# Three of the four input pairs of the Fox value projection computed as seven block products each

## The chip, the cores and the metric

The kernel runs on one core of one Trainium2 chip. The metric is the device time of one execution in microseconds (us); lower is better. Engines are named PE (TensorE, matrix products), DVE (VectorE), ACT (ScalarE), POOL (GpSimd) and SP (the engine that issues most transfers).

## What is computed

Two transformer blocks run on 256 tokens of width 1024. The change lies in the second block's first mixer, the "Fox" attention, whose projection gives queries, keys, values, a forget logit and a gate:

```
q, k, v, f_logit, gate = _split(x @ w_in, [H * dh, H * dh, H * dh, H, D])   # H = 8, dh = 128, D = 1024
...
s = jnp.einsum('bqhd,bshd->bhqs', q_b, k).astype(jnp.float32) * scale
s = s + jnp.transpose(c_b, (0, 2, 1))[..., None] - cum_t[:, :, None, :]
s = jnp.where(kpos[None, :] <= qpos[:, None], s, -jnp.inf)
p = jax.nn.softmax(s, axis=-1).astype(v.dtype)
return jnp.einsum('bhqs,bshd->bqhd', p, v)
```

All inputs are float32. The value projection is v = x @ w_v with x 256 x 1024 and w_v 1024 x 1024.

## The kernel before

**Precision.** A float32 operand is split into a rounded part ("high", type fp32r) and the remainder ("low"). One block product is three matmuls (`three`, L484 to L486): high x high, high x low, low x high, each 128 x 128 by 128 x 512.

**Weight chunks.** Weights come as chunks of 128 partitions x 2048 floats (1 MB) through a ring of four slots, `raw`. For chunk c ACT writes the high part `whi` (`hi(c)`, L1219), then DVE writes the low part `wlo` (`lo(c)`, L1679); POOL does the low parts of the output projection's chunks (L1611). PE waits in `take(c)` for the low part. SP may load chunk c once the low part of chunk c - 4 is done, and ACT may write `whi` of c once PE has used c - 4. Every engine runs its instructions in the order written; semaphores tie the engines together.

**The stage.** The query and key chunks Q0 to Q7 (`C_FQK + h`), one head each, take 32 matmuls of 512 columns and 16 of 256 columns on PE (L519, L525) into two of four banks (4 to 7) of PSUM, so head h uses the banks of head h - 2. After each, ACT copies the right halves of both banks into `qk_sum` ("cross copy", L1460) and makes one high part; DVE adds the left halves (L2038), writes q and k (L2040, L2041) and makes one low part, of the chunk four ahead. PE starts head h only when DVE's addition of head h - 2 is done (`qk2_ready`). Then come the four value chunks (`C_FV`, 24 matmuls each in `by_tokens`), with the score matmuls of heads 0 and 1 (`scores2`, L962) ahead of the last. ACT and DVE copy the values out, scaled by the rows' norm (L1464, L1469, L2047). DVE also adds the mask to the attention bias (L2056). In the attention, for each head, PE makes scores, DVE adds the bias and takes the row maximum (`causal`, L1862), ACT takes the exponential (`exps`, L1345), PE transposes (`turn_probs`, L782), DVE copies (L1870) and PE multiplies with the values (L837 to L839). Then the output projection begins (`C_FO`).

**Seven products, as used already.** In both feed-forward down projections ten weight chunks are done by Strassen's scheme in seven block products instead of eight (`seven`). The sums of weight blocks are written by DVE (`weight_sums`, L366 to L370) into the next ring slot, so that a pair of inputs takes two slots, the second of them without a load. The first slot needs only 1536 of its 2048 columns split.

## Time and profile before

| | us |
|---|---|
| median of 3 runs | 701.61 |
| lowest, highest | 700.35, 701.9 |
| profiled execution | 700.18 |
| its span, first to last instruction | 698.4 |
| PE busy in the span | 689.4 |
| DVE busy | 544.3 |
| ACT busy | 399.2 |

The profile is of one execution. A busy time counts an instruction from its start to its end. Matmuls overlap, so that the pace is read from start to start, not from durations. "Idle before" names what released an engine. The mean granted clock of PE was 0.997 of 2.4 GHz.

### The profile page before, as it was taken

What the parts mean: (1) busy time and instruction counts of PE and PEld (TensorE: products, weight loads), DVE (VectorE), ACT (ScalarE), POOL (GpSimd) and SP (SyncE); (2) the same over time, 40 slices, a digit from 0 to 9 for tenths busy, and PEclk for the clock granted to TensorE, in tenths of its full rate; (3) what the DMA queues carried; (4) which work ended last, traced back from release to release, by engine and by line L of the source; (5) the groups of instructions that cost most, each with busy time, mean ns of one, the idle gap of its engine ahead of it and who ended that gap; (6) DMA issues with size and microseconds to landing.
All of it is one profiled execution on the core that took longest, in us unless ns stands there. A gap on an engine that the chain in (4) does not pass through costs nothing.

```text
span 698.4 us, 9915 instructions
## 1 busy us (share of the span) xinstructions
PE 689.4 (99%) x3702; PEld 588.1 (84%) x3702; DVE 544.3 (78%) x808; ACT 399.2 (57%) x533; POOL 84.4 (12%) x70
## 2 busy tenths in 40 slices
PE   8999999999999999999999999999999999999995
PEld 7888888888888788888888888888888888888885
DVE  6788788999777776877778999976763748898757
ACT  6866555556377546655555556487444625576451
POOL 0022204000000000022104000000006172140001
PEclk9999999999999999999999999999999999999998
DMA  8966653356685053755553347664663174543001
GB/s 341 367 229 232 227 193 120 121 181 242 249 330 203 1 218 152 262 181 182 184 186 139 110 172 301 234 249 173 234 249 116 74 292 133 173 158 137 1 1 60
DMA packets 21253, 129.34 MB, mean 185 GB/s; under 512 B 2520, under 2 KB 3936, under 8 KB 7008
## 3 DMA queue, kind: packets, MB, share of 16 engines
q1 hardware_dynamic: 19872, 127.51, 49.8%
q10 hardware_dynamic: 1344, 1.34, 0.6%
q8 instruction: 23, 0.38, 0.2%
q14 instruction: 14, 0.11, 0.0%
HBM read 127.79 MB, written 1.06 MB: 184 GB/s over the span
## 4 chain that ended last, share of the span: by engine, by line
PE 97%; DVE 1%; DMA 1%; issue 0%; ACT 0%; ACTq 0%; DVEq 0%
PE ps L519 25%; PE ps L484 16%; PE ps L486 16%; PE ps L485 16%; PE ps L525 13%; PE ps L504 1%; PE ps L782 1%; PE ps L678 1%; PE ps L538 1%; PE ps L1142 1%; PE ps L962 1%; PE ps L508 1%; DMA raw<-in_first 1%; PE ps L694 1%; PE ps L837 1%; PE ps L839 1%
## 5 line engine op out<-in xcount | busy, mean ns | idle before, releaser
L1219 ACT ACTIVATE whi<-raw 128x2048 fp32r<-128x2048 f32 (+1 forms) x88 | 164.6, 1873 | 69.4 <-PE ps L486 51.1
L1679 DVE TENSOR_TENSOR wlo<-raw,whi 128x2048 fp32r<-128x2048 f32 (+1 forms) x81 | 181.2, 2255 | 17.5 <-ACT whi L1219 17.4
L519 PE MATMUL ps<-xt,whi 128*128 128x512 f32 x752 | 180.1, 391 | 0.0
L519 PEld LDWEIGHTS ps<-xt,whi 128*128 128x128 f32 x752 | 138.1, 188 | 26.7
L484 PE MATMUL ps<-whi,xt 128*128 128x512 f32 (+2 forms) x340 | 134.7, 396 | 0.0
L486 PE MATMUL ps<-whi,xt 128*128 128x512 f32 (+2 forms) x340 | 130.1, 383 | 0.0
L485 PE MATMUL ps<-wlo,xt 128*128 128x512 f32 (+2 forms) x340 | 129.9, 382 | 0.0
L525 PEld LDWEIGHTS ps<-xt,wlo 128*128 128x128 f32 x752 | 96.4, 191 | 3.7
L525 PE MATMUL ps<-xt,wlo 128*128 128x256 f32 x752 | 97.5, 283 | 0.0
L484 PEld LDWEIGHTS ps<-whi,xt 128*128 128x128 f32 x340 | 64.0, 188 | 14.1 <-issue 2.4
L486 PEld LDWEIGHTS ps<-whi,xt 128*128 128x128 f32 x340 | 63.9, 188 | 12.7
L1773 DVE TENSOR_TENSOR wlo<-raw,whi 128x2048 fp32r<-128x2048 f32 x32 | 73.3, 2290 | 1.0
L485 PEld LDWEIGHTS ps<-wlo,xt 128*128 128x128 f32 x340 | 64.1, 188 | 11.4 <-issue 0.2
L1263 ACT ACTIVATE work<-ps 128x512 f32<-128x512 f32 x44 | 26.1, 596 | 71.9 <-PE ps L519 71.6
L1302 ACT ACTIVATE whi<-raw 128x2048 fp32r<-128x2048 f32 x32 | 61.1, 1909 | 0.0
L1620 POOL TENSOR_TENSOR XN<-work 128x128 f32<-128x128 f32 x8 | 20.4, 2550 | 328.6 <-DVE work L1731 328.6
L1611 POOL TENSOR_TENSOR wlo<-raw,whi 128x2048 fp32r<-128x2048 f32 (+1 forms) x7 | 31.8, 4550 | 167.8 <-ACT whi L1219 167.8
L486 PE MATMUL ps<-whi,h_low 128*128 128x512 f32 x126 | 49.0, 389 | 0.0
L1720 DVE TENSOR_TENSOR work<-ps,work 128x512 f32<-128x512 f32 x44 | 30.2, 688 | 18.0 <-ACT work L1263 17.8
L484 PE MATMUL ps<-whi,h_high 128*128 128x512 f32 x88 | 34.2, 389 | 0.0
L485 PE MATMUL ps<-wlo,h_high 128*128 128x512 f32 x88 | 34.2, 389 | 0.0
L1726 DVE TENSOR_TENSOR work<-work 128x512 f32<-128x512 f32 x44 | 30.3, 692 | 1.8 <-ACT work L1252 0.4
(267 smaller groups left out, 838.9 us busy)
## 6 DMA issues: line engine op xcount, KB each, us to landing
raw<-in_gu SPq DMA_DIRECT2D x41, 1024.0 KB, 4.8
raw<-in_dn SPq DMA_DIRECT2D x22, 1024.0 KB, 4.7
raw<-in_win SPq DMA_DIRECT2D x8, 1024.0 KB, 6.3
raw<-in_fqk SPq DMA_DIRECT2D x8, 1024.0 KB, 4.8
raw<-in_wout SPq DMA_DIRECT2D x4, 1024.0 KB, 4.8
raw<-in_fg SPq DMA_DIRECT2D x4, 1024.0 KB, 5.7
raw<-in_fv SPq DMA_DIRECT2D x4, 1024.0 KB, 4.8
raw<-in_fo SPq DMA_DIRECT2D x4, 1024.0 KB, 4.8
```

What stands on the lines that cost most here:

```text
L484: pe.matmul(o, xh, wh, start=start, stop=False, skip_group_check=more)
L485: pe.matmul(o, xh, wl, start=False, stop=False, skip_group_check=more)
L486: return pe.matmul(o, xl, wh, start=False, stop=stop, skip_group_check=more)
L519: return pe.matmul(ps[:, banks[u], :], wh[:, k * S + u * P:k * S + (u + 1) * P], x, start=k == 0, stop=k == KD - 1)
L525: pe.matmul(ps[:, banks[u], S:2 * S], wl[:, k * S + u * P:k * S + (u + 1) * P], xth[:, k, :], start=False, stop=False)
L1219: act.activation(whi[:, c % RING, w], raw[:, c % RING, w], ACT.Copy).then_inc(hi_ready, 1)
L1302: act.activation(whi[:, c % RING, :], raw[:, c % RING, :], ACT.Copy).then_inc(hi_ready, 1)
L1611: pool.tensor_tensor(wlo[:, c % RING, 0:n], raw[:, c % RING, 0:n], whi[:, c % RING, 0:n].bitcast(F32), ALU.subtract).then_inc(lo_ready, 1)
L1679: dve.tensor_tensor(wlo[:, c % RING, w], raw[:, c % RING, w], whi[:, c % RING, w].bitcast(F32), ALU.subtract).then_inc(lo_ready, 1)
L1720: dve.tensor_tensor(g, ps[:, 2 * i:2 * i + 2, 0:S], g, ALU.add).then_inc(gu_read, 1)
L1726: dve.tensor_tensor(g, g, ffn_row.unsqueeze(1).broadcast_to([P, 2, S]), ALU.mult).then_inc(gate_scaled, 1)
L1773: dve.tensor_tensor(wlo[:, c % RING, :], raw[:, c % RING, :], whi[:, c % RING, :].bitcast(F32), ALU.subtract).then_inc(lo_ready, 1)
```

## The change

The value weights are laid out anew: four chunks, each with two blocks of 128 input rows (a pair) and all 1024 outputs. Pairs 0 to 2 take two ring slots each (V0 to V5: V0, V2 and V4 loaded, V1, V3 and V5 written by `weight_sums`), and pair 3 is slot V6, done in eight products. So there are seven value slots instead of four chunks, `C_FV + 0` to `C_FV + 6`.

- PE: three times 21 matmuls (`v_seven`: 9 on the first slot, 12 on the second) and 24 (`v_eight`, with the scores of heads 0 and 1 after its first 12), 87 instead of 96. Banks 4 to 7 (`SHARED` on) collect the four products that go to more than one output block or have to be combined, banks 0 to 3 the rest of the four output blocks. The score banks of heads 0 and 1 are now 6 and 7, free after DVE's second combining addition; heads 4 on use banks 2 and 3; the transposed probabilities use banks 0 and 1, so the first transpose waits for both copies out of them.
- DVE, in the query and key steps: after head 0, 1 and 2 the input sums (`v_input_sums`: one 128x512 and four 128x128 operations), a head later their low part (`v_sums_lo`), after heads 4, 5 and 7 the weight sums. After head 7: the low parts of V4, V5, V6, four combining additions (`v_shared`), and two operations for each half of the values instead of one.
- ACT: after the high part of heads 0, 1 and 2 it waits for the input sums and rounds them; three more high parts; one copy and four scalings of the combined products; the high parts of the output projection's chunks 0, 1 and 2 (O0, O1, O2) stand elsewhere around them.

In the diff, names and lines are those of the changed program.

```diff
 
 
+V7 = 3
+V_SLOTS = KD // 2 + V7
+
+
...
-SKIP = {C_DN[f] + place(g): BANK for f in range(2) for g in SEVEN}
+TWICE = [C_DN[f] + place(g) for f in range(2) for g in SEVEN] + [C_FV + 2 * j for j in range(V7)]
+SUMS = [c + 1 for c in TWICE]
+SKIP = {c: BANK for c in TWICE}
 
...
+        v_in = view(work, 4096, 2 * S, "p (k s) -> p k s", k=2)
+        v_sums = view(work, 4096 + 2 * S, 3 * BANK, "p (j n) -> p j n", j=3)
...
+
+                c = C_FV + 2 * j
+                first, last = j == 0, j == V7 - 1
+
+                def summed(i):
+                    at = slice(i * P, (i + 1) * P)
+                    return hth[:, j, at], htl[:, j, at]
+
+                def product(bank, x, c, i, start, stop):
+                    w = slice(i * BANK, (i + 1) * BANK)
+                    return three(ps[:, bank, :], *x, whi[:, c % RING, w], wlo[:, c % RING, w], start, stop)
+
+                take(c)
+                product(SHARED, v_given(j, 0, 0), c, 1, first, last)
+                product(v_bank(0, 0), v_given(j, 1, 0), c, 3, first, False)
+                pe.wait_ge(ss_lo, 2 * NS + j + 1)
+                product(v_bank(0, 1), summed(3), c, 2, first, False).then_inc(chunk_used, 1)
+                take(c + 1)
+                product(SHARED + 1, summed(0), c + 1, 0, first, last)
+                if first:
+                    pe.wait_ge(qk2_ready, 3 * H2)
+                product(SHARED + 2, summed(1), c + 1, 2, first, last)
+                product(SHARED + 3, summed(2), c + 1, 1, first, last)
+                product(v_bank(1, 0), v_given(j, 1, 1), c + 1, 3, first, False).then_inc(chunk_used, 1)
+
+            def v_eight(p, between):
+
+                wh, wl = take(C_FV + V7 + p)
+                for nb in range(2):
+                    for t in range(NT):
+                        for k in range(2):
+                            w = slice(k * D + nb * BANK, k * D + (nb + 1) * BANK)
+                            m = three(ps[:, v_bank(t, nb), :], *v_given(p, k, t), wh[:, w], wl[:, w], p == V7 and k == 0 and t == nb == 1, p == KD // 2 - 1 and k == 1)
+                    if nb == 0 and between:
+                        m.then_inc(v_left, 1)
+                        between()
+                m.then_inc(chunk_used, 1)
...
+            def scores_early():
+
+                pe.wait_ge(p_sum, 8 + 2)
+                scores2(0)
+                scores2(1)
+
             pe.wait_ge(gate_ready, 4)
-            for i in range(3):
-                if i == 2:
-                    pe.wait_ge(qk2_ready, 3 * H2)
-                by_tokens(C_FV + i, (i % 2) * HALF, HALF, BANK, [2 + i // 2 * 4, 3 + i // 2 * 4], i % 2 == 0, i % 2 == 1)
-            scores2(0)
-            scores2(1)
-            by_tokens(C_FV + 3, HALF, HALF, BANK, [6, 7], False, True)
-            pe.wait_ge(v_act, 1)
-            pe.wait_ge(v_dve, 1)
+            pe.wait_ge(qk2_ready, 3 * (H2 - 2) + 1)
+            for j in range(V7):
+                v_seven(j)
+            for p in range(V7, KD // 2):
+                v_eight(p, scores_early if p == KD // 2 - 1 else None)
+            pe.wait_ge(v_dve, 2)
...
-            hi(C_FV + 1 + RING)
-            act.activation(v2[:, 0, 0:BANK], ps[:, 2, :], ACT.Copy, scale=rstd[:, 0:1]).then_inc(v_act, 1)
-            hi(C_FV + 2 + RING)
+                if h < V7:
+                    act.wait_ge(s_sum, 8 * NS + 5 * (h + 1))
+                    act.activation(hth[:, h, :], v_sums[:, h, :], ACT.Copy).then_inc(ss_hi, 1)
+            for c in range(C_FQK + H2 + RING, C_FO + 1):
+                hi(c)
+            act.wait_ge(chunk_used, C_FV + 2 * V7)
+            act.activation(v2[:, 0, 0:BANK], ps[:, SHARED, :], ACT.Copy).then_inc(p1_copied, 1)
+            for n, t, nb in ((1, 0, 0), (3, 1, 0), (4, 0, 1), (4, 1, 1)):
+                act.wait_ge(p_sum, 8 + n)
+                v = v2[:, t, nb * BANK:(nb + 1) * BANK]
+                act.activation(v, v, ACT.Copy, scale=rstd[:, t:t + 1]).then_inc(v_act, 1)
+            hi(C_FO + 1)
             exps(1, 0)
             exps(1, 1)
-            act.wait_ge(chunk_used, C_FV + 4)
-            act.activation(v2[:, 0, BANK:D], ps[:, 6, :], ACT.Copy, scale=rstd[:, 0:1]).then_inc(v_act, 1)
+            hi(C_FO + 2)
             for h in range(2, H2):
                 exps(1, h)
...
             dve.wait_ge(f_log, 1)
             dve.tensor_tensor_scan(ncum, fl, fl, zero[0:H2, :], ALU.add, ALU.bypass).then_inc(cum_ready, 1)
+            def v_input_sums(j):
+
+                k = slice(2 * j, 2 * j + 2)
+                (a11, a21), (a12, a22) = ([v_in[:, n, t * P:(t + 1) * P] for t in range(NT)] for n in range(2))
+                s1, s2, s3, s4 = (v_sums[:, j, i * P:(i + 1) * P] for i in range(4))
+                ready = 8 * NS + 5 * j
+                dve.tensor_tensor(v_in, xth[:, k, :].bitcast(F32), xtl[:, k, :].bitcast(F32), ALU.add).then_inc(s_sum, 1)
+                dve.wait_ge(s_sum, ready + 1)
+                dve.tensor_tensor(s1, a21, a22, ALU.add).then_inc(s_sum, 1)
+                dve.tensor_tensor(s3, a11, a21, ALU.subtract).then_inc(s_sum, 1)
+                dve.wait_ge(s_sum, ready + 2)
+                dve.tensor_tensor(s2, s1, a11, ALU.subtract).then_inc(s_sum, 1)
+                dve.wait_ge(s_sum, ready + 4)
+                dve.tensor_tensor(s4, a12, s2, ALU.subtract).then_inc(s_sum, 1)
+
+            def v_sums_lo(j):
+
+                dve.wait_ge(ss_hi, 2 * NS + j + 1)
+                dve.tensor_tensor(htl[:, j, :], v_sums[:, j, :], hth[:, j, :].bitcast(F32), ALU.subtract).then_inc(ss_lo, 1)
...
+
             for h in range(H2):
                 dve.wait_ge(chunk_used, C_FQK + h + 1)
                 bank = 4 + 2 * (h % 2)
...
+                    weight_sums(dve, C_FV)
+                lo(C_FQK + h + RING)
+                if h < V7:
+                    v_input_sums(h)
+                if 1 <= h <= V7:
+                    v_sums_lo(h - 1)
+                for j in range(1, V7):
+                    if h == 3 + 2 * j:
+                        weight_sums(dve, C_FV + 2 * j)
+
+            def v_shared():
+
+                dve.wait_ge(chunk_used, C_FV + 2 * V7)
+                dve.wait_ge(p1_copied, 3)
+                v = [[v2[:, t, nb * BANK:(nb + 1) * BANK] for nb in range(2)] for t in range(NT)]
+                dve.tensor_tensor(v[0][1], ps[:, SHARED + 2, :], v[0][0], ALU.add).then_inc(p_sum, 1)
+                dve.wait_ge(p_sum, 8 + 1)
+                dve.tensor_tensor(v[1][0], ps[:, SHARED + 3, :], v[0][1], ALU.add).then_inc(p_sum, 1)
+                dve.wait_ge(p_sum, 8 + 2)
+                dve.tensor_tensor(v[1][1], v[1][0], ps[:, SHARED + 1, :], ALU.subtract).then_inc(p_sum, 1)
+                dve.tensor_tensor(v[0][1], v[0][1], ps[:, SHARED + 1, :], ALU.subtract).then_inc(p_sum, 1)
 
             def values_out(nb):
-                dve.wait_ge(chunk_used, C_FV + 2 * nb + 2)
-                dve.tensor_scalar(v2[:, 1, nb * BANK:(nb + 1) * BANK], ps[:, 3 + 4 * nb, :], rstd[:, 1:2], None, ALU.mult).then_inc(v_dve, 1)
+
+                if nb:
+                    dve.wait_ge(chunk_used, C_FV + V_SLOTS)
+                else:
+                    dve.wait_ge(v_left, 1)
+                for t in range(NT):
+                    dve.wait_ge(v_act, 2 * nb + t + 1)
+                    v = v2[:, t, nb * BANK:(nb + 1) * BANK]
+                    dve.scalar_tensor_tensor(out=v, in0=ps[:, v_bank(t, nb), :], scalar=rstd[:, t:t + 1], in1=v, op0=ALU.mult, op1=ALU.add).then_inc(v_dve, 1)
 
             def causal(h):
-                masked(1, h, lambda t: bias2[:, h, 0:P] if t == 0 else bias2[:, h, P:3 * P])
-
+                masked(1, h, lambda t: bias2[:, h, 0:P] if t == 0 else bias2[:, h, P:3 * P], fox_scores(h))
+
+            lo(C_FQK + H2 + RING)
             dve.wait_ge(cst_landed, 16)
             dve.wait_ge(cum_spread, 32)
             diagonal_mask = mask[:, P:2 * P].unsqueeze(1).broadcast_to([P, H2, P])
             for to, of in ((0, P), (2 * P, 2 * P)):
                 dve.tensor_tensor(bias2[:, :, to:to + P], bias2[:, :, of:of + P], diagonal_mask, ALU.add).then_inc(f_order, 1)
             dve.wait_ge(f_order, 6)
+            for c in range(C_FQK + H2 + RING + 1, C_FO):
+                lo(c)
+            v_shared()
...
+    a["fg"] = blocks(g, HALF, BANK)
+    v = v.reshape(KD // 2, 2, P, 2, BANK).transpose(0, 2, 1, 3, 4).copy()
+    v[:V7] = v[:V7, :, :, ::-1].copy()
+    a["fv"] = v.reshape(KD // 2, P, SLOT)
     a["fo"] = halves_first(i["fox_w_out_2"])
...
```

**ACT, heads 0 to 2.** The order of its instructions there, before (L1460 is the cross copy, L1219 the high part of a chunk):

```order
L1219 ACTIVATE whi<-raw 128x2048 [waits chunk_used,raw_landed0]
L1460 ACTIVATE work<-ps 128x512 [waits chunk_used]
L1219 ACTIVATE whi<-raw 128x2048 [waits chunk_used,raw_landed1]
L1460 ACTIVATE work<-ps 128x512 [waits qk2_ready,chunk_used]
L1219 ACTIVATE whi<-raw 128x2048 [waits chunk_used,raw_landed2]
```

And with the change (L1537 is the cross copy, L1296 the high part, L1541 the rounding of the input sums):

```order
L1296 ACTIVATE whi<-raw 128x2048 [waits chunk_used,raw_landed0]
L1541 ACTIVATE hth<-work 128x512 [waits s_sum]
L1537 ACTIVATE work<-ps 128x512 [waits chunk_used]
L1296 ACTIVATE whi<-raw 128x2048 [waits chunk_used,raw_landed1]
L1541 ACTIVATE hth<-work 128x512 [waits s_sum]
L1537 ACTIVATE work<-ps 128x512 [waits qk2_ready,chunk_used]
```

The cross copy of heads 1 to 3 now stands behind a rounding that waits for DVE's input sums of the head before.

**DVE, after head 7's additions.** Before (L2056 is the mask addition, L2047 a copy out of values, L1862 the bias and maximum of head 0):

```order
L1679 TENSOR_TENSOR wlo<-raw,whi 128x2048 [waits hi_ready]
L2056 TENSOR_TENSOR gains<-gains,cst 128x8x128 [waits cum_spread,cst_landed]
L2056 TENSOR_TENSOR gains<-gains,cst 128x8x128
L2047 TENSOR_SCALAR work<-ps,st 128x512 [waits chunk_used,f_order]
L1862 ISA work,st<-ps,gains 128x128 [waits s_psum_1]
```

With the change (L1763 are the low parts of V3, V4, V5 and V6, L397 to L401 the weight sums of V5, L2188 the mask addition, L2162 on the combining):

```order
L1763 TENSOR_TENSOR wlo<-raw,whi 128x2048 [waits hi_ready]
L397 TENSOR_TENSOR raw<-raw 128x1024 [waits w_sum,lo_ready,raw_landed0]
L399 TENSOR_TENSOR raw<-raw 128x512 [waits w_sum]
L401 TENSOR_TENSOR raw<-raw 128x512 [waits w_sum]
L1763 TENSOR_TENSOR wlo<-raw,whi 128x1536 [waits hi_ready]
L2188 TENSOR_TENSOR gains<-gains,cst 128x8x128 [waits cum_spread,cst_landed]
L2188 TENSOR_TENSOR gains<-gains,cst 128x8x128
L1763 TENSOR_TENSOR wlo<-raw,whi 128x2048 [waits hi_ready,f_order]
L1763 TENSOR_TENSOR wlo<-raw,whi 128x2048 [waits hi_ready]
L2162 TENSOR_TENSOR work<-ps,work 128x512 [waits p1_copied,chunk_used]
L2164 TENSOR_TENSOR work<-ps,work 128x512 [waits p_sum]
```

Weight sums, three low parts and the combining now stand between the last head and the first maximum, and the mask addition stands ahead of the low part of V5.

**ACT, at the start of the attention.** Before (L1464 a copy out of values, L1345 the exponentials of heads 0 and 1):

```order
L1219 ACTIVATE whi<-raw 128x2048 [waits chunk_used,raw_landed1]
L1464 ACTIVATE work<-ps,st 128x512
L1219 ACTIVATE whi<-raw 128x2048 [waits chunk_used,raw_landed2]
L1345 ACTIVATE work,st<-work,st 128x128 [waits neg_ready_1]
L1345 ACTIVATE work,st<-work,st 128x256 [waits neg_ready_1]
```

With the change (L1545 and L1549 copy and scale the combined products, the L1296 rows are O1 and O2, L1422 the exponentials):

```order
L1545 ACTIVATE work<-ps 128x512 [waits chunk_used]
L1549 ACTIVATE work<-work,st 128x512 [waits p_sum] x4
L1296 ACTIVATE whi<-raw 128x2048 [waits chunk_used,raw_landed0]
L1422 ACTIVATE work,st<-work,st 128x128 [waits neg_ready_1]
L1422 ACTIVATE work,st<-work,st 128x256 [waits neg_ready_1]
L1422 ACTIVATE work,st<-work,st 128x128 [waits neg_ready_1]
L1422 ACTIVATE work,st<-work,st 128x256 [waits neg_ready_1]
L1296 ACTIVATE whi<-raw 128x2048 [waits chunk_used,raw_landed1]
```

One high part now stands between the scalings and the first exponential, and one between the exponentials of heads 1 and 2.

## Rows read from the trace of the kernel before

**Rows 1.** The page: busy time by engine, and the chain that ended last, by engine.

```profile
PE 689.4 (99%) x3702; PEld 588.1 (84%) x3702; DVE 544.3 (78%) x808; ACT 399.2 (57%) x533; POOL 84.4 (12%) x70
...
PE 97%; DVE 1%; DMA 1%; issue 0%; ACT 0%; ACTq 0%; DVEq 0%
```

**Rows 2.** Timeline, TensorE: start us, busy us, engine, line, out<-in, count [idle before].

```profile
509.29 2.08 PE L525 MATMUL ps<-xt,wlo 128*128 128x256 f32 x16
...
514.86 2.08 PE L525 MATMUL ps<-xt,wlo 128*128 128x256 f32 x16
...
519.97 0.39 PE L484 MATMUL ps<-whi,xt 128*128 128x512 f32 x1
...
536.29 1.47 PE L962 MATMUL ps<-work 128*128 128x128 f32 x8
537.41 0.58 PE L484 MATMUL ps<-whi,xt 128*128 128x512 f32 x1
...
543.10 0.49 PE L782 MATMUL ps<-eye,work 128*128 128x128 f32 x3
...
545.75 0.52 PE L782 MATMUL ps<-eye,work 128*128 128x128 f32 x3
```

**Rows 3.** Timeline, VectorE, in the query and key steps.

```profile
484.46 0.69 DVE L2038 TENSOR_TENSOR work<-ps,work 128x512 f32<-128x512 f32 x1 [0.81 <-ACT work L1460]
...
486.20 2.29 DVE L1679 TENSOR_TENSOR wlo<-raw,whi 128x2048 fp32r<-128x2048 f32 x1 [0.25 <-ACT whi L1219]
488.41 0.68 DVE L2038 TENSOR_TENSOR work<-ps,work 128x512 f32<-128x512 f32 x1
...
489.80 2.29 DVE L1679 TENSOR_TENSOR wlo<-raw,whi 128x2048 fp32r<-128x2048 f32 x1
493.04 0.69 DVE L2038 TENSOR_TENSOR work<-ps,work 128x512 f32<-128x512 f32 x1 [0.95 <-ACT work L1460]
...
524.81 2.35 DVE L2056 TENSOR_TENSOR gains<-gains,cst 128x1024 f32<-128x1024 f32 x2
```

**Rows 4.** Timeline, ScalarE, in the query and key steps and at the first two heads.

```profile
486.77 0.60 ACT L1460 ACTIVATE work<-ps 128x512 f32<-128x512 f32 x1 [0.60 <-PE ps L519]
487.26 1.91 ACT L1219 ACTIVATE whi<-raw 128x2048 fp32r<-128x2048 f32 x1
...
538.37 0.39 ACT L1345 ACTIVATE work<-work,st 128x128 f32<-128x128 f32 x1
...
539.25 0.39 ACT L1345 ACTIVATE work<-work,st 128x128 f32<-128x128 f32 x1
...
544.61 0.40 ACT L1345 ACTIVATE work<-work,st 128x128 f32<-128x128 f32 x1 [0.63 <-DVE st L1862]
```

**Rows 5.** Groups by line and shape, whole span: count, busy us, mean ns, idle before.

```profile
L1726 DVE TENSOR_TENSOR work<-work 128x512 f32<-128x512 f32 x44 | 30.3, 692 | 1.8 <-ACT work L1252 0.4
...
L1679 DVE TENSOR_TENSOR wlo<-raw,whi 128x1536 fp32r<-128x1536 f32 x8 | 14.0, 1752 | 0.0
...
L2177 DVE TENSOR_TENSOR work<-work 128x128 f32<-128x128 f32 x2 | 0.6, 293 | 0.1
```

**Rows 6.** Groups by line and shape, ScalarE: the rounding of a 128x512 sum.

```profile
L1267 ACT ACTIVATE hth<-work 128x512 fp32r<-128x512 f32 x6 | 3.8, 625 | 4.9 <-DVE work L1731 4.9
```

**Rows 7.** Timeline, VectorE, at the first weight sums of the first down projection.

```profile
135.09 1.22 DVE L366 TENSOR_TENSOR raw<-raw 128x1024 f32<-128x1024 f32 x1
...
137.68 0.68 DVE L1737 TENSOR_TENSOR h_low<-work,hth 128x512 fp32r<-128x512 f32 x1
```

**Rows 8.** The page: POOL's low parts; DMA issues, with us to landing.

```profile
L1611 POOL TENSOR_TENSOR wlo<-raw,whi 128x2048 fp32r<-128x2048 f32 (+1 forms) x7 | 31.8, 4550 | 167.8 <-ACT whi L1219 167.8
...
raw<-in_fv SPq DMA_DIRECT2D x4, 1024.0 KB, 4.8
```

**Rows 9.** Stretches at the end: length, busy us per engine, granted clock, DMA.

```profile
691.00:691.50 0.50, 0.25 (x3) 0.05 (x1) 0.47 (x2) 0.00 (x0) 0.50 (x1) 1.00 0.10 33
...
693.50:694.00 0.50, 0.00 (x0) 0.00 (x0) 0.46 (x1) 0.00 (x0) 0.00 (x0) 0.92 0.48 176
```

80 lines of the change are left out of this document (44 added, 36 removed).

## The prediction, before the result

> **What bounds the kernel now.** I read the busy times and the chain first: PE is busy in 689.4 of 698.4 us and makes up 97% of the chain [rows 1]. So a matmul taken away is worth its pace, as long as no other engine becomes late; an engine that makes PE wait costs the wait in full. The timeline of PE gives the paces. The value step starts at 519.97 and its first 72 matmuls end at 536.29, so one costs 16.32 / 72 = 0.227 us. The scores of two heads take 1.12 (to 537.41), the last 24 matmuls 5.69 (to 543.10). A query and key head takes 5.57 (509.29 to 514.86) [rows 2]. Counted back from 519.97, head 3 starts at 492.13 and head 4 at 497.70.
>
> Then I read what DVE and ACT do beside it, by the start of one instruction to the start of the next. A head's addition and its two products take 1.39 (488.41 to 489.80), the addition alone 0.68, a low part 2.21 (486.20 to 488.41) [rows 3]: 3.6 in a period of 5.57, so some 2 us are free per head. Head 1's addition can start at 488.41 only, since head 0's was late (484.46).
>
> **The change part by part, PE.** Nine matmuls fewer: 9 x 0.227 = **-2.04 us**. That is all there is to win.
>
> **DVE's added work** between 484.46 and the low part of V5:
> - input sums of a pair: one 128x512 addition of 0.69 [rows 5], 0.73 with the wait behind it; then four 128x128 of 0.29 [rows 5]. The last two wait each for the one before, the others follow each other 0.08 before the end, as elsewhere: 0.21 + 0.21 + 0.32 + 0.29 = 1.03. Together 1.76, three times.
> - their low part, a 128x512: 0.61, three times.
> - weight sums: 2.59 (135.09 to 137.68) [rows 7], three times.
> - low parts: ten instead of eight up to V5's, three of them 1536 wide (1.75 [rows 5], 1.67 from start to start): 7 x 2.21 + 3 x 1.67 against 8 x 2.21, 2.8 more.
>
> That is 5.3 + 1.8 + 7.8 + 2.8 = 17.7 us, where 8 heads had 8 x (5.57 - 3.6) = 16 free. But the order matters more than the total, so I lay the instructions one behind the other.
>
> **First place, heads 1 to 5.** ACT's rounding of the input sums waits for DVE, and the cross copy of the next head stands behind it, for which DVE waits in turn. DVE starts the input sums of pair 0 at 488.41 and ends them at 490.17. ACT rounds (0.62 [rows 6], 0.52 to the next start) to 490.74, cross copies (0.60 [rows 4]) to 491.36. DVE starts head 1's addition at 491.46 (before: 488.41). The copy's successor, the high part, starts 0.49 after it (486.77 to 487.26) and takes 1.91 [rows 4], so it ends at 493.16. The low part runs from 493.19 to 495.40, the sums of pair 1 to 497.16, and rounding and copy hold head 2's addition until 498.42 (before: 493.04 [rows 3]). It ends at 499.11. With 0.05 for the signal PE can start head 4 at 499.16 instead of 497.70: it **waits 1.46 us**. The same round, 6.96 us against PE's 5.57, brings head 3's addition to an end at 506.07, and head 5, due at 504.73, **waits 1.39 us**. The rounds have no more sums after that, and head 6 and 7 find their banks free.
>
> **Second place, heads 4 to 7 and the value step.** From 509.93 DVE is never idle. Head 4: 1.39 + 2.59 + 1.67, to 515.6. Head 5: 1.39 + 2.21 + 0 + 2.59, to 521.8. Head 6: 1.39 + 1.67, to 524.86. PE ends head 7 at 519.97 + 1.46 + 1.39 = 522.82. Its second product in V1, 12 matmuls later, waits for all of head 7's results, which are there at 524.86 + 1.53 = 526.39, where PE comes at 525.55: **0.84 us**. DVE goes on: low part of V3 to 528.5, weight sums to 531.06, low part of V4 to 532.73, mask addition (2.35 [rows 3]) to 535.1, low part of V5 to 537.39. PE, with 0.84 behind it, does the rest of V1, V2, V3 and V4 (9 + 9 + 12 + 9 matmuls = 8.84) and wants V5 at 535.23: **2.16 us**. The four waits make 5.85. A check by the other way: without any of them V5 would start 51 matmuls behind 519.97, at 531.53, and DVE gives it at 537.42, **+5.89 us**. That DVE's chain is what counts shows in this: shifting a wait from one place to another leaves 537.42 as it is.
>
> The transfers hold nobody: V4's slot is free after 515.6, 4.8 us to landing [rows 8] make 520.4, and it is wanted at 528.5.
>
> **Third place, the attention's start.** After V5 PE has 12 + 12 + 12 matmuls and the scores: 8.16 + 1.12, to 546.70. V5's products are there at 540.34; ACT copies to 540.93; DVE adds twice, to 542.44, ahead of the scores at 542.86, so no wait there, by 0.4. DVE's third and fourth addition and the two copies out end at 545.11, and the maxima of heads 0 and 1 at 546.4. ACT scales until 545.0 and then makes the high part of O1, 1.9 us, to 546.78, before the first exponential. In the trace the transpose follows the exponential's start by 1.14 (544.61 to 545.75) [rows 2, 4], so the first is at 547.83: **1.13 us** of waiting. Before, the exponentials began at 538.37 [rows 4], 4.7 us ahead of the transpose, and hid everything. ACT ends head 1's exponential (0.88 a head, 538.37 to 539.25 [rows 4]) at 548.45, makes the high part of O2 to 550.27, and starts head 2's exponential; its transpose is at 551.41. PE's other work (transpose, scores, transpose, values, scores: 2.65, from 543.10 to 545.75 [rows 2]) would allow 550.48: **0.93 us**. From there the heads run as before, since DVE, ACT and PE are all shifted alike; I know no slack that gives it back. POOL's low parts of O0 to O2, 4.55 us each [rows 8], end near 556; they are wanted from 560 on.
>
> **The sum:** -2.04 + 5.89 + 1.13 + 0.93 = +5.91; laid against the transpose of head 2, at 551.41 instead of 545.75, it is 5.66, since the 0.25 us that PE lost at the change from scores to values [rows 2] I had left out of the new count. It may come back, so **+5.7 to +5.9**; I take 5.7. The profiled execution took 700.18, so it becomes 705.9; it lies 1.4 under the median of the runs, 701.61, from which I forecast 701.6 + 5.7 = **707.3**.
>
> Both ends of what the trace of before does not show: the small sums at most 0.29 each without overlap and at least 0.21, three times 0.3 us; the handing over between DVE and ACT 0.03 to 0.10 at twelve places, 0.8 us; a landing of the mask's source late, none to 1 us; the first exponential 0 to 2.1 us late as O1's high part falls before or behind it. Together 705.0 to 709.3.
>
> **The rivals.**
> 1. *Faster.* The change as its plan has it: DVE's and ACT's additions fit under PE, and PE gains 2.04: 699.6. This decides at two points: the low part of V5 by 531.5, and the first exponential by 539.7, 1.14 ahead of the transpose that would then be due at 531.53 + 9.28 = 540.81. For it speaks that 16 of the 17.7 us were idle before; against it the rounds of 6.96 us, and weight sums and mask addition in a row. Chance 0.05.
> 2. *No difference.* DVE is in time (the rounds overlap more than I read), but the attention's start is not: -2.04 + 1.13 + 0.93 = 0: 701.6. Chance 0.06.
> 3. *The attention's start is covered*, DVE's chain is late: -2.04 + 5.89 = +3.6 to 3.9: 705.3. For it: ACT might take O1's high part while DVE still copies. Against it: the maxima are ready before ACT. Chance 0.08.
> 4. *The clock falls.* At the end of the kernel PE's last matmul lies in the stretch 691.0 to 691.5, and the granted clock is below 1.00 in 693.5 to 694.0 [rows 9], after some 2.3 us of standstill; my longest wait is 2.16, and waits of 1 to 1.4 us stand around it. If it falls to the lower level (1.2 GHz) until the 24 matmuls of V5 and the first half of V6 are done, these take twice 5.44: +5.7 + 5.4: 712.7. Chance 0.06.
>
> By the Trainium skill, page "TensorE: Matmul & The Clock Gate", section "Part 1: The HAM clock gate", an idle TensorE is put back to 1.2 GHz and gets its full rate only after it has been busy again. The trace shows the fall at the kernel's end; the way back up is in no row here.
>
> **How the numbers follow.** The forecast has 0.75; with rivals 3 and 4 that gives slower 0.89. Rival 2 is "same" (0.06, within 0.2%, about what a measurement of this kernel can tell), rival 1 is "faster" (0.05). The range is the forecast's own and rival 3's, with 0.7 us at either end for the scatter of the median that the sum is laid against (700.35 to 701.9): 704.3 to 710.0; rivals 1, 2 and 4, 0.17 together, stay outside.
>
> **What would show it.** PE's timeline: gaps of 1.4 us before heads 4 and 5, 0.8 in V1 and 2.2 before V5, none before V2, V3, V4, V6. DVE without idle time from 510 to 539.5, with ACT's rounding and cross copy as the releaser at heads 1 to 3. The first exponential behind a high part, at 546.7. The granted clock at 1.00 throughout. It is wrong if the low part of V5 ends before 535, if heads 4 and 5 start 5.57 after their predecessors, or if the heads of the attention gain back what their start lost.

## The result and the profile after

The changed kernel takes 707.19 us (median; 706.7 to 709.34), the kernel before, run beside it, 700.3 us (699.87 to 701.9). One execution more of the changed kernel, a slow one at 1401.31 us, is left out of its range and of the ratio; without it the median is 707.02. The ratio is 1.0100, with a 95% interval of 1.0088 to 1.0112: slower by 1%, at the place and by the waits that were forecast, and besides by a fall of TensorE's clock that was not. The forecast was 707.3 us; but the difference is 6.9 us (6.7 against 707.02) where the sum said 5.7, and the forecast time came out this close by luck: it was laid against a median (701.61) 1.3 us above what the kernel before took in all later runs.

The profiled execution of the changed kernel took 709.34 us, with a span of 707.6. Of that, 1.86 us were lost at the very start of the kernel, far from the change (the first matmul group of the Fox heads starts at 477.30 instead of 475.44). So 1.86 has to be taken off each time of this trace before it is laid beside [rows 2 to 4].

The page, its busy rows and the head of its chain, beside [rows 1]. PE is busy in fewer per cent, and VectorE has come into the chain with 6%:

```profile
PE 692.1 (98%) x3693; PEld 588.9 (83%) x3693; DVE 566.8 (80%) x844; ACT 407.2 (58%) x542; POOL 84.3 (12%) x70
PE 88%; DVE 6%; ACT 3%; issue 1%; DMA 1%; ACTq 0%; DVEq 0%
```

The timeline of PE after the change (start, duration, engine, line, operation, count, and in brackets the idle time before it and what ended it), cut to the groups behind an idle time and a few that give paces:

```profile
494.65 2.07 PE L556 MATMUL ps<-xt,wlo 128*128 128x256 f32 x16
501.04 0.70 PE L550 MATMUL ps<-xt,whi 128*128 128x512 f32 x2 [1.12 <-DVE work L2142]
501.58 2.07 PE L556 MATMUL ps<-xt,wlo 128*128 128x256 f32 x16
...
507.99 0.70 PE L550 MATMUL ps<-xt,whi 128*128 128x512 f32 x2 [1.14 <-DVE work L2142]
...
524.76 0.39 PE L515 MATMUL ps<-whi,xt 128*128 128x512 f32 x1
...
527.25 0.39 PE L517 MATMUL ps<-whi,htl 128*128 128x512 f32 x1
528.13 0.50 PE L515 MATMUL ps<-whi,hth 128*128 128x512 f32 x1 [0.49 <-DVE work L2145]
...
536.88 0.39 PE L517 MATMUL ps<-whi,htl 128*128 128x512 f32 x1
539.19 0.67 PE L515 MATMUL ps<-whi,hth 128*128 128x512 f32 x1 [1.92 <-DVE wlo L1763]
539.65 0.63 PE L516 MATMUL ps<-wlo,hth 128*128 128x512 f32 x1
540.08 0.63 PE L517 MATMUL ps<-whi,htl 128*128 128x512 f32 x1
...
542.64 0.46 PE L517 MATMUL ps<-whi,htl 128*128 128x512 f32 x1
...
551.48 0.52 PE L813 MATMUL ps<-eye,work 128*128 128x128 f32 x3 [0.87 <-ACT work L1422]
...
555.04 0.52 PE L813 MATMUL ps<-eye,work 128*128 128x128 f32 x3 [0.73 <-ACT work L1422]
```

All six waits stand where the prediction put them, and there is no other in this stage. And one thing is there that it gave only 0.06: from 539.19 to 542.64 eight matmuls start 0.43 us apart, not 0.227. The granted clock by stretches (PE's busy time and count, granted clock, share and rate of the transfers) shows why:

```profile
538.50:539.50 1.00, 0.31 (x1) 0.93 0.12 49
539.50:542.50 3.00, 3.00 (x8) 0.50 0.83 254
542.50:543.50 1.00, 1.00 (x5) 0.86 1.00 418
543.50:546.00 2.50, 2.50 (x13) 1.00 0.87 367
```

The clock fell to its lower level, 1.2 GHz, just behind the wait before V5, and came back to 2.4 GHz some 3.4 us later. The mean of 0.93 in the first stretch puts the fall at 539.36, 0.17 us after V5's first matmul has begun; the 0.86 in the third puts the return at 542.78. It cost 3.45 - 8 x 0.227 = 1.6 us.

VectorE and ScalarE in heads 0 and 1, and ScalarE at the attention's start, beside [rows 3, 4]: the rounding (L1541) stands ahead of the cross copy (L1537), the addition of head 1 waits for that, and the high part of O1 stands ahead of the first exponential.

```profile
491.72 0.29 DVE L2131 TENSOR_TENSOR work<-work 128x128 f32<-128x128 f32 x1
493.27 0.69 DVE L2142 TENSOR_TENSOR work<-ps,work 128x512 f32<-128x512 f32 x1 [1.26 <-ACT work L1537]
...
500.20 0.69 DVE L2142 TENSOR_TENSOR work<-ps,work 128x512 f32<-128x512 f32 x1 [0.65 <-ACT work L1537]
```

```profile
492.05 0.63 ACT L1541 ACTIVATE hth<-work 128x512 fp32r<-128x512 f32 x1 [4.02 <-DVE work L2131]
492.58 0.58 ACT L1537 ACTIVATE work<-ps 128x512 f32<-128x512 f32 x1
...
548.56 1.90 ACT L1296 ACTIVATE whi<-raw 128x2048 fp32r<-128x2048 f32 x1
550.37 0.39 ACT L1422 ACTIVATE work<-work,st 128x128 f32<-128x128 f32 x1
```

The round of heads 1 to 3 is 500.20 - 493.27 = 6.93 us; 6.96 were forecast.

### The profile page after: what moved, and what is told of

The parts are those of the page before. It is cut to its first block, busy times and chain, and to the rows that moved or that the text cites. A ratio compares the mean times of both kernels' runs of the same rounds, so it can differ in the third digit from the quotient of the medians.

```text
span 707.6 us, 9954 instructions
## 1 busy us (share of the span) xinstructions
PE 692.1 (98%) x3693; PEld 588.9 (83%) x3693; DVE 566.8 (80%) x844; ACT 407.2 (58%) x542; POOL 84.3 (12%) x70
## 4 chain that ended last, share of the span: by engine, by line
PE 88%; DVE 6%; ACT 3%; issue 1%; DMA 1%; ACTq 0%; DVEq 0%
PE ps L550 21%; PE ps L515 15%; PE ps L516 14%; PE ps L517 14%; PE ps L556 11%; DVE wlo L1763 2%; ACT whi L1296 1%; PE ps L535 1%; PE ps L709 1%; PE ps L813 1%; PE ps L1219 1%; PE ps L569 1%; PE ps L539 1%; DMA raw<-in_first 1%; PE ps L725 1%
## 5 line engine op out<-in xcount | busy, mean ns | idle before, releaser
L1296 ACT ACTIVATE whi<-raw 128x2048 fp32r<-128x2048 f32 (+2 forms) x91 | 168.8, 1861 | 65.2 <-PE ps L517 42.1
L1763 DVE TENSOR_TENSOR wlo<-raw,whi 128x2048 fp32r<-128x2048 f32 (+1 forms) x84 | 186.4, 2238 | 16.8 <-ACT whi L1296 16.7
L515 PE MATMUL ps<-whi,xt 128*128 128x512 f32 (+2 forms) x325 | 128.8, 396 | 0.0
L517 PE MATMUL ps<-whi,xt 128*128 128x512 f32 (+2 forms) x325 | 124.2, 382 | 0.0
L516 PE MATMUL ps<-wlo,xt 128*128 128x512 f32 (+2 forms) x325 | 124.1, 382 | 0.0
L515 PEld LDWEIGHTS ps<-whi,xt 128*128 128x128 f32 x325 | 61.2, 188 | 13.6 <-issue 2.4
L517 PEld LDWEIGHTS ps<-whi,xt 128*128 128x128 f32 x325 | 61.1, 188 | 12.1
L516 PEld LDWEIGHTS ps<-wlo,xt 128*128 128x128 f32 x325 | 61.3, 188 | 10.8 <-issue 0.2
```

What stands on the lines that cost most here:

```text
L515: pe.matmul(o, xh, wh, start=start, stop=False, skip_group_check=more)
L516: pe.matmul(o, xh, wl, start=False, stop=False, skip_group_check=more)
L517: return pe.matmul(o, xl, wh, start=False, stop=stop, skip_group_check=more)
L1296: act.activation(whi[:, c % RING, w], raw[:, c % RING, w], ACT.Copy).then_inc(hi_ready, 1)
L1763: dve.tensor_tensor(wlo[:, c % RING, w], raw[:, c % RING, w], whi[:, c % RING, w].bitcast(F32), ALU.subtract).then_inc(lo_ready, 1)
```

## The experiments

**The theory** is the prediction's: PE waits at three places, each for its own reason: ScalarE's rounding ahead of the cross copy (heads 4 and 5, and by it V1), VectorE's row of weight sums, mask addition and low parts (V5), and ScalarE's work ahead of the exponentials (the attention's start). **The rival** is that VectorE as a whole is too busy, so that a wait taken away at one place comes back at the next. The first four kernels, e1 to e4, undo one cause each and then all three; they were run beside the kernel before at 700.3 us, e5 to e8 at 700.24, e9 to e11 at 700.39 and e12 at 700.3.

### e1: the sums rounded one head later

```diff
                 hi(C_FQK + h + RING)
-                if h < V7:
-                    act.wait_ge(s_sum, 8 * NS + 5 * (h + 1))
-                    act.activation(hth[:, h, :], v_sums[:, h, :], ACT.Copy).then_inc(ss_hi, 1)
+                if 1 <= h <= V7:
+                    act.wait_ge(s_sum, 8 * NS + 5 * h)
+                    act.activation(hth[:, h - 1, :], v_sums[:, h - 1, :], ACT.Copy).then_inc(ss_hi, 1)
```

> One edit to the changed kernel: ScalarE rounds the input sums of pair h only after the cross copy and the high part of head h + 1, so no cross copy stands behind them. Theory A (two engines wait for each other in heads 1 to 3, and VectorE's chain alone sets the start of V5): the 4 us of VectorE's waiting there go, heads 4 and 5 start without a gap, V5's low part comes 3.9 us earlier, with a wait of some 1.9 us left before V5: 707.2 - 3.9 = 703.3. Theory B (the mere amount of VectorE's work is what is late): the gaps move from heads 4 and 5 to V1 and V5, and V5 starts as late as now: 707 to 706.5.

Measured: 702.57 us, ratio 1.0043 (1.0028 to 1.0057). PE's timeline, all its waits:

```profile
533.83 0.50 PE L515 MATMUL ps<-whi,hth 128*128 128x512 f32 x1 [2.11 <-DVE wlo L1763]
544.52 0.52 PE L813 MATMUL ps<-eye,work 128*128 128x128 f32 x3 [0.88 <-ACT work L1422]
548.08 0.52 PE L813 MATMUL ps<-eye,work 128*128 128x128 f32 x3 [0.72 <-ACT work L1422]
```

The waits of heads 4 and 5 and of V1 are gone, with the same work on every engine: an order of two instructions made them, not VectorE's load. The other three are as they were. The wait before V5 is 2.11 us, even a little longer, but behind it the matmuls of this execution go on at 0.23 us and the granted clock stays at 1.00: the clock didn't fall. The five executions lie in two groups, three at 702.3 to 702.6 us with a mean granted clock of 0.997, and two at 704.2 and 704.4 with 0.995 and 0.994. Two losses are about as large as this step of 1.8 us: the fall behind V5 (1.6), and the loss at the kernel's start that the changed kernel's profiled execution had (1.86). The lower mean speaks for the fall, since 3.4 us at half the clock take 0.0024 off the mean of 700 us, while the traces of e7, e8 and e11, which have the loss at the start alone, have a mean of 0.997 to 0.998. But neither of the two executions was profiled. If it is the fall, it came in the smaller part of e1's executions, and so the median lies below both expectations.

### e2: the mask addition behind the low parts of V5 and V6

```diff
-            diagonal_mask = ...
-            for to, of in ((0, P), (2 * P, 2 * P)):
-                dve.tensor_tensor(bias2[...], bias2[...], diagonal_mask, ALU.add).then_inc(f_order, 1)
             for c in range(C_FQK + H2 + RING + 1, C_FO):
                 lo(c)
+            diagonal_mask = ...
+            for to, of in ((0, P), (2 * P, 2 * P)):
+                dve.tensor_tensor(bias2[...], bias2[...], diagonal_mask, ALU.add).then_inc(f_order, 1)
```

> One edit to the changed kernel: VectorE adds the mask after the low parts of V5 and V6 instead of before V5's. Theory A (V5 waits for the low part behind the mask addition): the gap before V5 (2.2 us) shrinks to about 0, against some 0.4 us new at the early scores: 705.0 to 705.4. If besides the clock falls at that gap in most executions of the changed kernel, as it did in the profiled one (eight matmuls at 0.43 instead of 0.23 us, 1.6 us), another 1.6 goes: 703.4 to 703.8, with a granted clock of 1.00 in the stretch behind V5's start. Theory B (V5 is held by something else, a load or ScalarE's high part): no change, 707.2.

Measured: 709.9 us, ratio 1.0134 (1.0118 to 1.0151), slower than the changed kernel, against every expectation. The wait before V5 is gone, but the early scores wait 4.51 us. Timelines of PE, VectorE and GpSimd:

```profile
545.13 2.93 PE L995 MATMUL ps<-work 128*128 128x128 f32 x8 [4.51 <-DVE work L2164]
547.50 0.99 PE L515 MATMUL ps<-whi,xt 128*128 128x512 f32 x1
548.28 0.63 PE L516 MATMUL ps<-wlo,xt 128*128 128x512 f32 x1
```

```profile
536.91 6.71 DVE L2190 TENSOR_TENSOR gains<-gains,cst 128x1024 f32<-128x1024 f32 x2
543.65 0.69 DVE L2162 TENSOR_TENSOR work<-ps,work 128x512 f32<-128x512 f32 x1
```

```profile
537.07 5.47 POOL L1695 TENSOR_TENSOR wlo<-raw,whi 128x2048 fp32r<-128x2048 f32 x1 [154.03 <-DVE wlo L1763]
```

The two halves of the mask addition take 6.71 us instead of 2.35 [rows 3]. In just this time GpSimd makes the low part of O0, and takes 5.47 us where it took 4.6. Both instructions read two operands in SBUF. The row looks as if the two engines had taken turns: half an addition (1.2), then GpSimd's low part (4.6), then the other half. And PE, standing for 4.5 us, lost its clock as well (a granted clock of 0.50 from 546 to 551). e5 tests what held the addition.

### e3: the exponentials first

```diff
+            hi(C_FO + 1)
             act.wait_ge(chunk_used, C_FV + 2 * V7)
             act.activation(v2[:, 0, 0:BANK], ps[:, SHARED ...
 ...
-            hi(C_FO + 1)
             exps(1, 0)
             exps(1, 1)
-            hi(C_FO + 2)
 ...
             load_table(ACT.Sqrt)
+            hi(C_FO + 2)
             hi(C_FO + 3)
```

> One edit to the changed kernel: ScalarE makes the high part of O1 before it copies the shared product, where it idles, and that of O2 after the last exponential. Theory A (the first and third exponential wait behind these high parts): the waits before the transposes of head 0 and 2 go from 1.1 and 0.9 to 0.2 and 0: 707.2 - 1.8 = 705.4. Theory B (VectorE's combining, copies and maxima hold the first exponential just as long): the transposes come no earlier, 707.2, or the high part of O2 is now late for the output projection and gives it back: 707 or more.

Measured: 712.88 us, ratio 1.0177 (1.016 to 1.0194). The waits of both transposes are gone, as meant. But O2's high part, and with it GpSimd's low part of O2, came some 12 us later. In the changed kernel the next three low parts stand apart; here GpSimd makes all four in one row, to 583.15, and the row ran into the layer norm. GpSimd, VectorE and PE:

```profile
564.88 18.27 POOL L1695 TENSOR_TENSOR wlo<-raw,whi 128x2048 fp32r<-128x2048 f32 x4 [16.08 <-ACT whi L1296]
584.73 4.88 POOL L1695 TENSOR_TENSOR wlo<-raw,whi 128x2048 fp32r<-128x2048 f32 x1 [1.58 <-ACT whi L1296]
```

```profile
581.59 2.12 DVE L2269 SCALAR_TENSOR_TENSOR X<-X,st,gains 128x512 f32<-128x512 f32 x1
...
583.82 0.75 DVE L2273 SCALAR_TENSOR_TENSOR X<-X,st,gains 128x512 f32<-128x512 f32 x1
...
585.27 4.89 DVE L2273 SCALAR_TENSOR_TENSOR X<-X,st,gains 128x512 f32<-128x512 f32 x1
```

```profile
584.63 0.66 PE L1094 MATMUL ps<-eye,X 128*128 128x128 f32 x4 [0.69 <-DVE X L2273]
590.22 1.12 PE L1094 MATMUL ps<-eye,X 128*128 128x128 f32 x4 [4.23 <-DVE X L2273]
```

The first of VectorE's four instructions, L2269 at 581.59, begins while the fourth low part still runs, and takes 2.12 us instead of 0.75. So VectorE is 1.4 us late, and its last one, L2273, falls behind GpSimd's next low part, which in the changed kernel begins only when that is done (587.79 there, VectorE's last from 586.95 to 587.70). The same instruction takes 0.75 us with GpSimd at rest and 4.89 beside its low part, and PE stands for 4.23 us. The granted clock of 590 to 600 is then 0.73. So the test of the exponentials was blurred by a collision of my own making; e6 repeats it without.

### e4: all three together

The three edits above in one kernel.

> The three edits together: rounding late, mask late, exponentials first. Theory A: VectorE gives V5's low part at the time TensorE wants it, no wait before V5, so also no fall of the clock, and some 0.8 us left before the first transpose: -2.04 + 0.8 = 1.2 us under the kernel before, 699.1. Theory B (the work added to VectorE does not fit in any order): a wait of 2 to 3 us stays before V5 or V6, 702 to 703.

Measured: 713.64 us, ratio 1.0185 (1.0168 to 1.0202). It has both collisions: PE waits 4.55 us at the early scores and 4.23 at the layer norm. Its expectation was the sum of three edits, each costed without GpSimd.

### e5: the mask addition late, GpSimd held until it is done

```diff
 # beside e2's edit
             sums(1)
+            pool.wait_ge(f_order, 6)
             for c in range(C_FO, C_DQ):
                 lo(c)
```

> Edit: the mask addition stands behind the low parts of V5 and V6, as in the run before (e2), and GpSimd's low parts of the output projection's chunks additionally wait until the mask addition is done. Theory (GpSimd's long low part, with both engines on SBUF operands, held up VectorE's mask addition: 6.71 us instead of 2.35): the addition takes 2.35 us again, TensorE's wait before V5 (1.92 on record plus the clock behind it, some 1.6) is gone, a wait of some 0.5 us is left before the early scores, and the first transpose waits some 1.7. That is 707.2 - 2.1 - 1.6 + 0.5 + 0.6 = 704.6 us; 706 if the clock behind V5 falls in few executions only. Rival (the addition is slow for its place, its data or the transfers around it): it stays near 6.7 us and the kernel near 709.9.

Measured: 704.64 us, ratio 1.0068 (1.0051 to 1.0085), 5.3 us better than e2 by one added line, GpSimd's wait. VectorE and GpSimd now, and PE's only wait in the value step behind V1:

```profile
537.37 2.36 DVE L2191 TENSOR_TENSOR gains<-gains,cst 128x1024 f32<-128x1024 f32 x2
```

```profile
539.80 4.61 POOL L1695 TENSOR_TENSOR wlo<-raw,whi 128x2048 fp32r<-128x2048 f32 x1 [156.32 <-DVE gains L2191]
```

```profile
541.23 1.58 PE L995 MATMUL ps<-work 128*128 128x128 f32 x8 [0.17 <-DVE work L2165]
```

The addition takes 2.36 us in the same place with the same data. So its length in e2 was GpSimd's doing. It also shows that the wait before V5 was VectorE's row with the mask addition in it, and that it is worth the wait and, as far as the sum tells, part of the clock behind it: of the 2.5 us gained over the changed kernel 2.1 are the wait, less 0.3 at the scores and 0.3 at the first transpose; 1.0 is left, and the clock's 1.6, in a part of the changed kernel's executions, is the one thing in sight to make it up. This last step is argued, not shown.

The Trainium skill's page "SBUF — State Buffer", section "SBUF: two separate sides", says of the port pair that the two engines share that it is an exclusive lock: of a GpSimd instruction and a VectorE instruction with two SBUF inputs the one that starts first has it to its end, and the other stands still. The traces agree (2.35 to 6.71 us; 0.75 to 4.89). VectorE's operations with an operand in PSUM are not touched: beside the GpSimd row above (539.80 to 544.41), in e5, the combining and the copies out (L2163 to L2179) keep their 0.68 to 0.70 us each, the first and the last of them here:

```profile
539.76 0.69 DVE L2163 TENSOR_TENSOR work<-ps,work 128x512 f32<-128x512 f32 x1
...
542.41 1.40 DVE L2179 SCALAR_TENSOR_TENSOR work<-ps,st,work 128x512 f32<-128x512 f32 x2
```

### e6: ScalarE's order, without the collision

```diff
 # behind the copy of the shared products
-            for n, t, nb in ((1, 0, 0), (3, 1, 0), (4, 0, 1), (4, 1, 1)):
-                ... scaling ...
-            hi(C_FO + 1)
-            exps(1, 0)
-            exps(1, 1)
-            hi(C_FO + 2)
+            hi(C_FO + 1)
+            hi(C_FO + 2)
+            scaled(1, 0, 0)
+            scaled(3, 1, 0)
+            exps(1, 0)
+            exps(1, 1)
+            scaled(4, 0, 1)
+            scaled(4, 1, 1)
 # VectorE
             v_shared()
-            values_out(0)
             causal(0)
             causal(1)
+            values_out(0)
```

> Edit: ScalarE makes the high parts of the output projection's chunks O1 and O2 directly behind the copy of the shared products, while it waits for the combining, and the scalings of the second half come behind the exponentials of heads 0 and 1; VectorE takes the maxima of heads 0 and 1 before the first copies out. Nothing else is moved, and no split is put off until the table load. Theory: the waits of the first transpose and of head 2's are ScalarE's row of work between the combining and the exponentials, so most of 1.13 + 0.93 us goes: 707.2 - 1.65 = 705.5 us, with the wait before V5 as it was and GpSimd's low parts in their old places. Rival (these waits are held by the maxima or by VectorE's combining, or another collision like that of the run with the exponentials first): 707 us or more.

Measured: 705.36 us, ratio 1.007 (1.0054 to 1.0087). The waits in its trace behind V5, all of them:

```profile
554.05 0.49 PE L868 MATMUL ps<-work 128*128 128x128 f32 x2 [0.33 <-DVE work L1960]
```

Both transposes are free. VectorE's order was changed too (the maxima ahead of the first copies out), but e3 moved only ScalarE's high parts, and the same two waits were gone there: so they were the order of ScalarE's work. What the changed kernel doesn't have is the small wait of head 1's products for VectorE's copy; e2 and e3 have it as well, with 0.50 us.

That the median is the expected 705.5 is luck in part. The wait before V5 is as it was (1.92 us), and the profiled execution, at 708.15 us, shows the fall of the clock behind it (0.50 from 540 to 542) and the loss at the kernel's start. The other three took 704.44 and 704.87 us with a mean clock of 0.999, and 705.84 with 0.996: it looks as if the fall came in some and not in others, and the median lies between.

### e7: the three repairs together

e1, e5 and e6 in one kernel.

> All together: the sums rounded a head later (e1), the mask addition behind the low parts with GpSimd held (as e5), ScalarE's order (as e6). Theory: of the 5.9 + 2.06 us of waits only some 0.3 before the scores and 0.3 at the first transpose are left, no fall of the clock, and the nine matmuls fewer (2.04) come through: 700.3 - 2.04 + 0.55 = 698.8 us, faster than both kernels. Rival (each repair moves the wait to the next engine, as in the four-fold run): 702 to 703 us or more.

Measured: 699.53 us, ratio 0.9992 (0.9982 to 1.0002), 7.7 us better than the changed kernel with the same arithmetic. Two waits are left:

```profile
539.78 1.58 PE L995 MATMUL ps<-work 128*128 128x128 f32 x8 [0.18 <-DVE work L2171]
547.64 0.49 PE L868 MATMUL ps<-work 128*128 128x128 f32 x2 [0.49 <-DVE work L1961]
```

It is 0.7 us above the expectation, and no faster than the kernel before beyond doubt. PE is later by more than these two waits say. From the value step's start, 522.01, the 75 matmuls ahead of the scores would take it to 539.03; the scores begin at 539.78, 0.75 late: 0.4 are lost at V5, whose low part VectorE begins at 531.52 after waiting 0.32 us for ScalarE's high part, and 0.3 at the scores, for VectorE's second combining addition behind the mask addition. And head 1's products begin 1.01 us behind head 2's transpose (546.63), where it was 0.36 before: 0.65 more. The second wait is in e8 as well.

### e8: one pair instead of three

```diff
-V7 = 3
+V7 = 1
```

> Edit: only the first of the three additional pairs is left in the seven-product scheme beside none other, that is, the value projection has one pair in seven products instead of three, so 93 matmuls against 96 of plain products, and no sums are made in heads 4 and 5. Theory (the loss is in the waits of heads 4 and 5, of V1 and of V5, which the second and third pair bring): three matmuls fewer than before are 0.68 us and nothing is paid: some 699.6 us. Rival (each pair costs its share of the loss): 700.3 + 6.9 / 3 = 702.6 us.

(It is the first of the four pairs that is computed in seven products here.) Measured: 700.48 us, ratio 1.0005 (0.9995 to 1.0014), nearer to the theory than to the rival. No wait is left in heads 4 to 7 and in the value step, but one behind it:

```profile
548.38 0.49 PE L868 MATMUL ps<-work 128*128 128x128 f32 x2 [0.50 <-DVE work L1954]
```

So even a single pair pays a fixed price at the attention's start. One cause was in sight: the kernel before has one copy out of the second half on VectorE there, 0.74 us, and ScalarE the other; the changed kernel has both on VectorE, 1.41.

### e9 and e10: these copies behind head 1's transposes

```diff
                 if h == 1:
                     causal(2)
+                if h == 2:
                     values_out(1)
```

e9 is e7 with it, e10 is e8 with it.

> Edit: as e7, and VectorE's copies out of the value projection's second half (two of 0.7 us, where the kernel before has one on VectorE) come behind the copy of head 1's transposes, not ahead of it. In e7 TensorE waited 0.49 us there, and head 1's products began 1.01 us behind the next transpose instead of 0.36. Theory (the row of work on VectorE, 0.66 us longer than before, holds them): that 0.65 us goes, 699.5 - 0.65 = 698.9 us, faster than before by 0.2%. Rival (something behind it, the exponentials of head 3 or the copies out, takes the time over): 699.5 us as e7.

> Edit: one pair in seven products (as e8), with the same move of the copies out as in e9. Theory: e8's three matmuls fewer (0.68 us) were given back by 0.65 us at head 1's products, where its trace shows a wait of 0.50 us; with the move 700.5 - 0.65 = 699.8 us. Rival: 700.5 us as e8.

Measured: 699.7 us, ratio 0.9986 (0.9977 to 0.9995), and 700.39 us, ratio 0.9996 (0.9987 to 1.0005). Neither gained over its model; e9 is faster than the kernel before by 0.14%. The wait has moved on by one head, from VectorE's copy to the exponential behind the next maximum, as e9's PE shows:

```profile
546.88 0.52 PE L813 MATMUL ps<-eye,work 128*128 128x128 f32 x3 [0.33 <-ACT work L1422]
```

### e11 and e12: two pairs, and the copies apart

e11 is e9 with two pairs (90 matmuls). e12 is e11 with one of the two copies in either place:

```diff
                 if h == 1:
                     causal(2)
+                    values_out(1, [0])
                 if h == 2:
-                    values_out(1)
+                    values_out(1, [1])
```

> Edit: all of e9 with two pairs in seven products, 90 matmuls. Theory (by then every pair pays its 0.68 us apart from the start of the scores, where VectorE's combining comes late): 698.9 + 0.68 - 0.4 = 699.2 us, since VectorE has 4.4 us less to do before the combining. Rival (each pair pays in full): 698.9 + 0.7 = 699.6 us; or (pairs pay nothing): 698.9 us.

> Edit: as e11 (two pairs, 90 matmuls), but of VectorE's two copies out of the second half one stands ahead of head 1's transposes, where the kernel before had its only one, and one behind them. Theory (the copies together are 1.4 us of VectorE's row at the attention's start, which held head 1's products by 0.65 us in e7 and head 3's exponentials and their transpose by 0.33 us and more in e9 and e11; split, each is small enough to fit): some 0.3 us better than e11, 699.1 us. Rival (VectorE has no slack anywhere in the first three heads, so 0.66 us more work there costs its length wherever it stands): 699.4 us as e11.

Measured: 699.42 us, ratio 0.9984 (0.9974 to 0.9994), and 699.53 us, ratio 0.9985 (0.9975 to 0.9995). Both are faster than the kernel before by 0.15%, and e11 has the lowest median of all, though e7, e9, e11 and e12 can't be told apart. So e11's time decides between none of its expectations (699.2, 699.6, 698.9). Its trace says more: its 78 matmuls from 522.04 end in scores at 539.72, without any delay, where e7 with three pairs was 0.75 us late. So with the third pair its 0.68 us are lost again between V5 and the scores, where VectorE is late. In e12 the transpose of head 3 waits just as in e9:

```profile
544.45 0.52 PE L813 MATMUL ps<-eye,work 128*128 128x128 f32 x3
...
546.78 0.52 PE L813 MATMUL ps<-eye,work 128*128 128x128 f32 x3 [0.33 <-ACT work L1422]
```

From head 2's transpose to head 3's it is 2.33 us, in the kernel before 1.78 (545.75 [rows 2] to 547.53). Head 2's transpose itself stands at 544.45, 1.30 us earlier than before, and 1.36 with the 0.06 by which the Fox heads start later in this trace (475.50 instead of 475.44): all that six matmuls are worth (1.36). 0.55 of it is lost at the next head. So for the last half microsecond the runs fit the rival, that in the first three heads VectorE has no slack and 0.66 us more work there costs about its length wherever it stands: in all three places that were tried, some 0.55 to 0.65 us went. That this work is the cause isn't shown, since no run gives one of the two copies back to ScalarE.

## Why the prediction was right, point by point

- *Nine matmuls fewer, -2.04.* Right in size: e12 shows 1.36 of 1.36 at head 2's transpose for six, and the changed kernel's matmuls keep the pace of 0.227 us outside the clock's fall.
- *Heads 4 and 5, 1.46 + 1.39.* Right. The value step starts at 524.76 - 1.86 = 522.90 instead of 519.97, 2.93 us late where 2.85 were forecast. e1 shows the cause: the rounding ahead of the cross copy.
- *V1, 0.84.* It was 528.13 - 527.25 - 0.23 = 0.65.
- *V5, 2.16.* It was 539.19 - 536.88 - 0.23 = 2.08. Cause shown by e5.
- *First transpose 1.13, head 2's 0.93.* Measured 1.03 and 0.91 (from the matmul behind the scores to the transpose 551.48 - 547.49 = 3.99, where e6, without a wait, takes 2.96; and 3.56 - 2.65). Cause shown by e3 and e6.
- *The 0.25 us that may come back.* Wrong: the prediction took 5.7 and not 5.9 in the hope that PE's loss at the change from scores to values would go. It is still there (the first matmul behind the scores takes 0.58 us at 547.49 as at 537.41 in [rows 2]). Without the clock, the way to head 2's transpose is 555.04 - 1.86 - 545.75 - 1.6 = 5.8 us longer.
- *The clock, rival 4.* The one step of weight that failed. The mechanism was named and given 0.06 at a price of 5.4 us beside a forecast with none. It happened in the profiled execution, at 1.6 us. The chance was too small: the row it rested on, read as a fall some 2.3 us after the last matmul [rows 9], lay close beside a wait forecast at 2.16, and the 1.92 us of standstill before V5 were enough. (That row was read a little short too: the last matmul ends at 691.26, and a mean of 0.92 in 693.5 to 694.0 puts the fall at 693.9, 2.7 us behind it.) The price was too high, since it let the lower level last for 24 matmuls, where it lasted for eight. How often it falls in the changed kernel isn't settled. The traces of e3 and e6 show it behind the same wait of 1.92 us, e1's doesn't behind 2.11. A changed kernel with neither this fall nor the loss at the start would take 709.34 - 1.86 - 1.6 = 705.9 us, and none of its other executions is below 706.7, which speaks for the fall in most of them.
- *The base.* 5.8 and 1.6 are 7.4, and the profiled execution, less its 1.86 at the start, is 7.3 above 700.18. The median is 6.9 above the later median of before. The absolute forecast hit by luck: a base 1.3 too high and an effect 1.2 too low cancelled.

The expectations of e2, e3 and e4 failed at one step that is in the prediction too: it called GpSimd's low parts harmless, since nobody wanted them before 560. It asked when their results were wanted, not what VectorE did meanwhile. In the changed kernel nothing came of it, because GpSimd's first low part waits for VectorE's last one and began at 541.42, just behind it, and VectorE's next work has an operand in PSUM.

## What to carry to other kernels

Of a plan that spares the bounding engine work by giving it to two others, lay their instructions one behind the other before building it: here 7.7 us came back with the same arithmetic, by order alone, in three places (a rounding ahead of a copy, a large addition ahead of a wanted low part, a split ahead of an exponential). Check each moved VectorE instruction with two SBUF operands against what GpSimd does in that time, and each wait of 2 us on TensorE for the clock behind it. What was left of the gain after all repairs was 0.7 us of 2.04 with three pairs and 1.0 of 1.36 with two: no order that was tried gave back the rest. In the traces of e7 and e12 it goes where TensorE comes to a row of VectorE's work that has just got longer.
